# Mean squares from one product each, and convolution taps moved to earlier columns of the input projection

## What is computed

```python
def rmsnorm(x, g):
    xf = x.astype(jnp.float32)
    y = xf * lax.rsqrt(jnp.mean(xf * xf, axis=-1, keepdims=True) + RMS_EPS)
    return (y * g).astype(x.dtype)

ux = modulate(rmsnorm(x, norm1_g[l]), sh1, sc1) @ w_in[l]       # and uc from ctx
...                                                            # conformer_conv: 31 taps, depthwise;
...                                                            # rwkv: shift of 3 taps, key norm, scans
x = x + gt1 * (mix_x @ w_out[l])
x = x + gt2 * swiglu(modulate(rmsnorm(x, norm2_g[l]), sh2, sc2), ffn_wg[l], ffn_wu[l], ffn_wd[l])
```

## Time and profile before

| | |
|---|---|
| median of three runs | 4800.23 us |
| the profiled execution, its own time | 4803.96 us |
| its span in the profile | 4801.8 us |
| PE busy | 4443.0 us (93%) |
| DVE busy | 2203.6 us (46%) |
| ACT busy | 1320.5 us (27%) |
| POOL busy | 113.4 us (2%) |
| mean granted clock of TensorE | 0.958 of full speed |

### The profile page before, as it was taken

One profiled execution on the slowest core, in us unless ns is written; L12 is line 12 of the kernel. 1 busy time (PEld: TensorE's weight loads), 2 busy tenths in 40 slices (PEclk: granted clock), 3 DMA queues, 4 the chain that ended last, 5 costly groups with the idle time before them and its releaser, 6 DMA issues.

```text
span 4801.8 us, 81633 instructions
## 1 busy us (share of the span) xinstructions
PE 4443.0 (93%) x35773; PEld 3088.1 (64%) x35773; DVE 2203.6 (46%) x2957; ACT 1320.5 (27%) x1698; POOL 113.4 (2%) x107
## 2 busy tenths in 40 slices
PE   6997998899999998899889979898799999999996
PEld 3556997488855554899478536444466666666664
DVE  1566775232200255677244010345266666666663
ACT  2023223100000113322110021144254444444441
POOL 0000000000000000000000000000200000000000
PEclk9998999999999998999999989899799999999998
DMA  5330000111111332000222214100389999999995
GB/s 206 141 122 28 4 4 30 53 53 62 63 43 53 132 132 105 3 4 4 75 76 97 79 69 158 70 1 9 111 302 350 350 349 351 348 348 350 349 343 169
DMA packets 115465, 671.66 MB, mean 140 GB/s; under 512 B 11472, under 2 KB 12496, under 8 KB 57072
## 3 DMA queue, kind: packets, MB, share of 16 engines
q1 hardware_dynamic: 102496, 610.68, 33.7%
q0 software_dynamic: 12672, 56.48, 4.2%
HBM read 637.62 MB, written 30.68 MB: 139 GB/s over the span
## 4 chain that ended last, share of the span: by engine, by line
PE 83%; DVE 9%; ACT 3%; DMA 3%; issue 1%; POOL 0%; SPq 0%; DVEq 0%; ACTq 0%; POOLq 0%
PE psum L723 57%; PE psum L1280 14%; PE psum L1295 9%; DVE work L1429 1%; DMA ring<-w_in 1%; DMA ring<-stream 1%; DVE xt L1621 1%; PE psum L1273 1%; PE psum L1168 1%; PE psum L1254 1%; PE psum L1264 1%; DVE work L1915 1%; DVE ht L1399 0%; POOL places L661 0%; DVE ring_parts L2018 0%
## 5 line engine op out<-in xcount | busy, mean ns | idle before, releaser
L723 PE MATMUL psum<-ht,ring 128*128 128x512 f32 (+3 forms) x2368 | 825.2, 509 | 27.3 <-ACT ht L2148 14.1
L723 PE MATMUL psum<-work 64*64 64x64 f32 (+3 forms) x12552 | 683.1, 240 | 48.9 <-ACT work L2255 18.6
L723 PEld LDWEIGHTS psum<-ht,ring 128*128 128x128 f32 (+2 forms) x2368 | 437.8, 186 | 412.4 <-issue 374.1
L723 PEld LDWEIGHTS psum<-work 64*64 64x64 f32 (+2 forms) x12552 | 527.3, 139 | 154.5 <-issue 84.0
L723 PE MATMUL psum<-work,ring 128*128 128x512 f32 (+2 forms) x1488 | 458.0, 469 | 15.4 <-DMA ring<-stream 8.2
L723 PE MATMUL psum<-work_parts,ahead_parts 128*128 128x512 f32 (+1 forms) x1056 | 379.8, 360 | 31.1 <-DVE ht_parts L1788 31.1
L723 PEld LDWEIGHTS psum<-work,ring 128*128 128x128 f32 (+1 forms) x1488 | 258.7, 197 | 212.6 <-issue 199.2
L723 PE MATMUL psum<-work_parts,ring_parts 128*128 128x512 f32 (+1 forms) x1056 | 378.9, 359 | 0.0
L723 PE MATMUL psum<-ht_parts,ahead_parts 128*128 128x512 f32 (+1 forms) x1056 | 377.9, 358 | 0.0
L1750 DVE SCALAR_TENSOR_TENSOR xt<-psum,mod,xt 128x512 f32<-128x512 f32 x40 | 32.8, 820 | 555.0 <-PE psum L723 555.0
L1280 PE MATMUL psum<-work_parts 128*128 128x512 f32 x1024 | 278.6, 393 | 0.0
(11 more groups left out here) (285 smaller groups left out, 5418.6 us busy)
## 6 DMA issues: line engine op xcount, KB each, us to landing
ring<-stream SPq DMA_DIRECT2D x192, 1024.0 KB, 5.0
ring<-w_in SPq DMA_DIRECT2D x192, 1024.0 KB, 6.9
ht<-w_in SPq DMA_DIRECT2D x64, 1024.0 KB, 4.8
ht<-w_out SPq DMA_DIRECT2D x64, 1024.0 KB, 7.8
ring<-w_out SPq DMA_DIRECT2D x64, 1024.0 KB, 7.4
xt_rows<-xt POOLq DMA_DIRECT2D x2, 3132.0 KB, 13.8
xt<-xt_rows POOLq DMA_DIRECT2D x2, 3132.0 KB, 10.6
xt<-x_cm SPq DMA_DIRECT2D x8, 256.0 KB, 9.7
```

The costliest lines, as they stand in the source:

```text
L723: mm = pe.matmul(*args, **kwargs)
```

## The change

The squares of a norm are added up on VectorE (`add_square`), tile by tile in place into the first square; the squares behind it alternate between two tiles of the same buffer. TensorE makes one product of the sum. By-tile norms add square k-1 after the update of tile k, and the last one behind it. At the first norm ScalarE makes the squares after the first modulation turn, ahead of its work for the second row. The squares of a norm with context are taken over a tile's whole 783 columns in one operation. `EARLY_TAPS` goes from 20 to 36; the remaining 84 taps are spread over raw columns 0 to 11, seven each, and columns 12 to 15 have none.

```diff
-EARLY_TAPS = 20
+EARLY_TAPS, TAP_COLUMNS = 36, 12
...
+        sums_of = {"ht": [ht[:, i, :] for i in range(3)], "mix": [sq_mix[:, i, :] for i in range(3)],
+                   "attn": [sq_attn[:, i, :] for i in range(3)]}
...
-            def mean_square(with_ctx, squares):
-                by_tile("act", [(Cn("mean_dm"), squares[:, k, :]) for k in range(KT)], sq_act, with_ctx)
+            def mean_square(with_ctx, place):
+                pe.wait_ge(sq_added, w.next(sq_added, KT - 1))
+                j, stands, n_stands = banks.place("act")
+                if stands:
+                    pe.wait_ge(freed[stands], n_stands)
+                px, pc = halves(j)
+                total = sums_of[place][0]
+                if with_ctx:
+                    matmul(pc, Cn("mean_dm"), cs(total), start=True, stop=True)
+                for c in (0, CTX):
+                    mm = matmul(px[:, c:c + CTX], Cn("mean_dm"), xs(total)[:, c:c + CTX], start=True, stop=True)
+                mm.then_inc(ready["act"], 1)
...
+            def add_square(k, place, with_ctx):
+                total, *squares = sums_of[place]
+                f = whole(with_ctx)
+                dve.wait_ge(sq_act, w.next(sq_act, 2 if k == 1 else 1))
+                tt(f(total), f(total), f(squares[k % 2]), ALU.add).then_inc(sq_added, 1)
+                dve.wait_ge(sq_added, w.next(sq_added))
...
-                conv_taps(layer, EARLY_TAPS + late * n // 16, EARLY_TAPS + late * (n + 1) // 16)
+                first, last = (EARLY_TAPS + late * min(m, TAP_COLUMNS) // TAP_COLUMNS for m in (n, n + 1))
+                conv_taps(layer, first, last)
...
-            def add_gated(gate, layer, with_ctx, permuted):
+            def add_gated(gate, layer, with_ctx, permuted, place):
...
                     dve.sem_inc(x_tile, 1)
+                    if k >= 2:
+                        add_square(k - 1, place, with_ctx)
+                add_square(KT - 1, place, with_ctx)
...
-            def norm(shift, layer, with_ctx, squares, final=False, by_tile=True, modulations=0):
+            def squares(place, with_ctx, by_tile=True):
+                total, *temps = sums_of[place]
+                f = whole(with_ctx)
                 for k in range(KT):
                     if by_tile:
                         act.wait_ge(x_tile, w.next(x_tile))
-                    for f, b in parts(with_ctx):
-                        ins = fn(f(squares[:, k, :]), f(xt[:, k, :]), ACT.Square)
-                    ins.then_inc(sq_act, 1)
+                    if k >= 3:
+                        act.wait_ge(sq_added, w.next(sq_added))
+                    fn(f(temps[k % 2] if k else total), f(xt[:, k, :]), ACT.Square).then_inc(sq_act, 1)
...
                 mod_turn(0, q)
+                if q == 0:
+                    act.wait_ge(x_updated, 1)
+                    squares("ht", True, by_tile=False)
```

More of the change, by code:

```diff
@@ L356, in build @@
         x_tile = sem("x_tile")
+        sq_added = sem("squares_added")
         std_ready = sem("std_ready")
@@ L489, in cs, with whole @@
             return t[..., 0:CTX]
+        def whole(with_ctx):
+            return (lambda t: t) if with_ctx else xs
         def parts(with_ctx):
@@ L1082, in _ @@
             for layer in range(2):
-                mean_square(True, ht)
+                mean_square(True, "ht")
                 input_projection(layer)
@@ L1091, in _ @@
                 output_projection(layer == 0)
-                mean_square(layer == 0, sq_mix)
+                mean_square(layer == 0, "mix")
                 feed_forward(layer == 0)
             else:
-                mean_square(False, ht)
+                mean_square(False, "ht")
             def mods_after(slot):
@@ L1331, in _ @@
             output_projection_2()
-            mean_square(False, sq_attn)
+            mean_square(False, "attn")
             routing()
@@ L1827, in _ @@
                 if layer == 0:
+                    for k in range(1, KT):
+                        add_square(k, "ht", True)
                     modulation(0, 0, 2)
@@ L1840, in _ @@
                 dve.wait_ge(restored, 16 * (layer + 1))
-                add_gated(2, layer, layer == 0, True)
+                add_gated(2, layer, layer == 0, True, "mix")
                 updated()
@@ L1844, in _ @@
                 feed_forward(layer)
-                add_gated(5, layer, layer == 0, False)
+                add_gated(5, layer, layer == 0, False, "ht")
             updated()
@@ L2081, in _ @@
             modulation(2, 2, 6)
-            add_gated(2, 2, False, False)
+            add_gated(2, 2, False, False, "attn")
             updated()
@@ L2130, in norm @@
                         act.wait_ge(x_tile, w.next(x_tile))
-                    for f, b in parts(with_ctx):
-                        ins = fn(f(squares[:, k, :]), f(xt[:, k, :]), ACT.Square)
-                    ins.then_inc(sq_act, 1)
+                    if k >= 3:
+                        act.wait_ge(sq_added, w.next(sq_added))
+                    fn(f(temps[k % 2] if k else total), f(xt[:, k, :]), ACT.Square).then_inc(sq_act, 1)
+                w.skip(sq_added, 2)
+            def norm(shift, layer, with_ctx, place=None, final=False, modulations=0):
+                if place:
+                    squares(place, with_ctx)
                 if modulations:
@@ L2345, in _ @@
                 mod_turn(0, q)
+                if q == 0:
+                    act.wait_ge(x_updated, 1)
+                    squares("ht", True, by_tile=False)
             for layer in range(2):
-                if layer == 0:
-                    act.wait_ge(x_updated, 1)
-                norm(0, layer, True, ht, by_tile=layer > 0, modulations=1 + layer)
+                norm(0, layer, True, "ht" if layer else None, modulations=1 + layer)
                 act.wait_ge(zeroed, w.next(zeroed))
@@ L2360, in _ @@
                     banks.pair("dve")
-                norm(3, layer, layer == 0, sq_mix)
+                norm(3, layer, layer == 0, "mix")
                 feed_forward(layer == 0)
@@ L2365, in _ @@
             else:
-                norm(0, 1, False, ht, final=True)
+                norm(0, 1, False, "ht", final=True)
             def mods_after(slot):
@@ L2539, in _ @@
             fn(lam[:, 2:4], lam[:, 0:2], ACT.Exp).then_inc(lam_exp, 1)
-            norm(0, 2, True, ht, modulations=2)
+            norm(0, 2, True, "ht", modulations=2)
             projections()
@@ L2544, in _ @@
                 banks.pair("dve")
-            norm(3, 2, False, sq_attn)
+            norm(3, 2, False, "attn")
             routing()
```

## The result

The changed kernel takes **4748.74 us** (median of 4 runs, 4745.4 to 4749.44) beside 4800.34 us for the kernel before on the same chip; the ratio is 0.9893, with a 95% interval from 0.9881 to 0.9906. That is 51.6 us less; 56.7 were forecast. The profiled execution has 4749.44 us of its own, 0.7 above its median, while that of before was 3.6 above its own (4803.96 against 4800.34); so the two spans differ by more than the medians, 54.5 us (4801.8 and 4747.3), and the following reading accounts for that difference.

The account below looks back on a forecast made before the run. TensorE, with 83% of the chain, was taken to bound the kernel, through its work and its waits. Norms 27.1, layer 0's columns 15.6 and layer 1's 14.0 sum to 56.7 us off 4800.2: 4743.5 us, range 4732 to 4761.

Parts of the forecast that it names:

- The first norm: First norm: squares paced by adds, second modulation turn late at the low clock, product ends at 59.2, not 65.3: gain 6.1 us.
- Adds: VectorE's adds of squares over 783 columns at norms with context: 1.02 us taken for each.
- Norms with context by tile: Layer 0's mix norm and layer 1's start: TensorE waits 3.4 us, short product 2.93 us; gains 4.0 and 4.1 us.
- Norms without context: Layer 1's mix norm, final norm, attention norm: wait 2.4 us, product about 1.1 us; 3.4 us each, 10.2 together.
- Early taps: Layer 0: 34 taps take 32.3 us and end before the next gated value is due; nothing waits, cost 0.
- Layer 0's columns: End of layer 0's projection: tapless columns 12 to 15 lose their waits, despite pauses at columns 8 and 10: gain 15.6 us.
- the first rival: Layer 0's added pauses at columns 8 and 10 lower the clock, 3.0 us each: gain 50.7, 4749.5 us; chance 0.10.
- Layer 1's columns: End of layer 1's projection: waits of 2.03 and 4.10 us and the low clock go: gain 14.0 us.
- The second rival: The key chain, not taps, sets TensorE's waits; only the last column's taps count: gain 38.5, 4761.7 us; chance 0.08.
- Nothing lost behind a norm: Stages behind each norm run no longer than before, loss 0; longer ones would show the prediction wrong.

Follow-up runs that it names:

- experiment 2: Kernel before the change with only the new spread of taps (36 early, 7 in each of columns 0 to 11), old norms: 4772.24 us.
- experiment 3: Changed kernel with ScalarE making the first norm's squares before the copies of both modulation rows: 4738.91 us.
- experiment 9: The changed kernel run once more, unaltered, in a later job: 4742.43 us.
- experiment 4: Changed kernel with 8 taps in each of columns 0 to 7 and 5 in 8 to 11, instead of 7 in all twelve: 4741.38 us.
- experiment 7: Changed kernel with 36 early taps but the other 84 spread over all 16 columns: 4764.88 us.
- experiment 10: The kernel of experiment 8 (changed kernel with 20 early taps, the rest in columns 0 to 11) run again beside the changed kernel: 4747.0 us.
- experiment 1: Changed kernel with the taps as before (20 early, the rest over 16 columns), so the norms alone: 4774.62 us.
- experiment 5: Changed kernel with the edits of experiment 3 and experiment 4 together: 4737.08 us.
- experiment 6: Kernel of experiment 5 plus two rounds of products of constants on TensorE while it waits at the five by-tile norms: 4738.54 us.
- experiment 8: Changed kernel with 20 early taps and the other 100 in columns 0 to 11 (8 or 9 each): 4746.16 us.
- experiment 11: The kernel of experiment 5 run again beside the changed kernel: 4736.0 us.

## Why the prediction was right

It gave 4743.5 us, from 4732 to 4761, and faster with a chance of 0.97; the two medians, 4748.7 and 4742.4, lie on both sides of it. The mechanism held stage by stage. That the total came so close is in part luck: the first norm and layer 0's columns gave 1.1 us more each and the second block's context came 2.1 sooner, while the three norms without context gave 2.1 less, layer 1's columns 0.7 less, and a stage with no edit in it lost 2.4. By its steps:

- **The first norm**, 6.1 forecast, 7.2 measured. The late turn at the low clock came as worked out (3.57 us where 3.6 stood). The adds paced ScalarE at 1.01 us and not 1.03, and its copies began at 50.51 us and not behind 51.2.
- **Adds.** 1.02 us was taken; the mean is 975 ns, and 1.0 in a chain. The waits of 3.44 and 2.5 to 2.8 us came where 3.4 and 2.4 were forecast.
- **Norms with context by tile**, 4.0 and 4.1 forecast, 4.6 and 4.2 measured: the mean product took 2.38 and 2.71 us, not the 2.93 that was taken, since the clock came down inside it (granted 1.00 until 915 us, 0.54 in the next).
- **Norms without context**, 10.2 forecast, 8.1 measured. This is the term that was sized wrongly. The step that failed is "about 1.1 us (two thirds of 1.56) at the full clock, since 2.4 is near 2.03": the product took 1.14, 1.72 and 2.07 us in the three, and the waits were 0.1 to 0.4 us longer than 2.4. The prediction had named this case ("At the low clock 0.9 less each").
- **Early taps**, cost 0 forecast. The 34 taps take 32.22 us (32.3 forecast) and end at 144.96, and the next gated value still waits for TensorE, not the reverse. Timeline of DVE after:

```profile
112.74 32.22 DVE L1456 SCALAR_TENSOR_TENSOR work<-work,vec 128x783 f32<-128x783 f32 x34
...
147.25 0.69 DVE L1443 TENSOR_TENSOR work<-psum,work 128x512 f32<-128x512 f32 x1 [2.29 <-PE psum L731]
```

- **Layer 0's columns**, 15.6 forecast, 16.7 measured. The pauses of 1.57 and 1.8 us came as 1.58 and 1.70 and left the clock up, as forecast, and so they did in the three other traces that have them (experiments 2, 3 and 9): the first rival falls. Counted from the projection's start, they delayed product 20 by 1.9 us and not by 2.75: TensorE came to the first of them 0.9 us sooner, as its first product took 22.57 us where that of before took 23.46, partly at the low clock. The rest, from product 22 to the recurrence, brought 8.2 us where 8.1 were forecast. The prediction takes the turn at 1.8 us where its row says 1.95; the stretch that it is part of, from the key product of column 12 to product 22, came out at the 5.15 us that were worked out.
- **Layer 1's columns**, 14.0 forecast, 13.3 measured: a wait of 0.59 us for the key sum stayed, where 0.2 was taken, and the first product took 22.94 us where it took 22.53 before.
- **The second rival**, a chain on ScalarE that paces the keys, falls by experiments 2, 4 and 7: with fewer taps ahead of them the keys' waits go, tap by tap.
- **Nothing lost behind a norm** was wrong. It was one of the prediction's own signs of being wrong ("if the stages behind each norm run longer than before"), and stages behind the norms lost some 5 us in the first pair of traces, of which 2.4 lie ahead of the mix norm of layer 0. The change touches nothing there. In the windows from TensorE's start behind its wait of 11.5 us to the first update of the output projection, of before, after, and experiment 10 (first column the window, PEclk the granted clock):

```profile
core 0: us, PE busy (x) PEld busy (x) DVE busy (x) ACT busy (x) POOL busy (x), PEclk, DMA share, GB/s
828.07:860.45 32.38, 31.22 (x81) 15.01 (x82) 12.03 (x24) 0.00 (x0) 0.00 (x0) 0.94 0.17 65
```

```profile
804.55:838.88 34.33, 33.17 (x81) 15.82 (x82) 12.12 (x25) 0.00 (x0) 0.00 (x0) 0.88 0.16 62
```

```profile
809.07:841.28 32.21, 31.05 (x81) 14.87 (x82) 12.03 (x24) 0.00 (x0) 0.00 (x0) 0.95 0.17 66
```

The same work takes 2 us more where the granted clock is 0.88 and not 0.94. Most of it is a second stretch at the low clock within the stage. All thirteen traces have a pause of 1.16 us there, ahead of the output projection's first product; behind it, before and after:

```profile
849.78:852.78 3.00, 3.00 (x7) 1.40 (x8) 0.00 (x0) 0.00 (x0) 0.00 (x0) 1.00 0.28 44
```

```profile
826.70:829.70 3.00, 3.00 (x4) 1.45 (x5) 0.00 (x0) 0.00 (x0) 0.00 (x0) 0.50 0.00 0
```

Of the thirteen traces three have the short form, 32.1 to 32.4 us (before, experiments 2 and 10), and ten the long one, 34.1 to 34.5 us (the changed kernel twice, experiments 1, 3 to 8 and 11). Experiments 8 and 10 are one kernel, so the form isn't fixed by the code. But both kernels with the old norms have the short one and ten of the eleven traces with the new norms the long one, so a part of the edit in it isn't excluded. Why the clock falls in one execution and not in another stays open, and so does the cause of the 1.3 us lost at the end.

The rule of the Trainium skill that was weighed (page "TensorE: Matmul & The Clock Gate", Part 1: an idle array falls to 1.2 GHz and gets 2.4 back after sustained work) would have put all seven products low if every pause counted as idle, as the prediction took it. The rows are between: all those with context came out low wholly or in part (2.38, 2.71, 2.91, 2.93 us against 1.56), of the three others one came out at the full clock (1.14 us).

## What to carry to other kernels

Where an engine off the path has slack, the question is not how much of it but where it stands when the path asks for it: the taps taken off the last 4 of 16 raw columns and put on the first 12 and further ahead were worth 30 us in two layers by the traces (16.7 + 13.3), with no work removed. Replacing long products by adds on another engine wins the products' length less the last two adds and one short product, often at the low clock. What the engines had done under the long product has to be looked at anew (here the modulation copies, 5.6 us). Check such edits of a few us in the trace, stage by stage: medians of one kernel differed by 6 us between jobs.

## What the runs showed of the hardware

- A pause of TensorE is priced twice, by its length and by the clock behind it, and its length alone doesn't tell the second. Pauses up to 2.03 us left the key products at 1.53 to 1.56 us in every trace; one of 2.91 gave 2.33; one of 3.46 gave 2.67 (2.93 in the repetition), and those of 4.92 and 4.94 gave 2.93. But the mean products without context, one form, took 1.14, 1.72 and 2.07 us behind 2.81, 2.49 and 2.48 us within one execution, and a pause of 1.16 us ahead of layer 0's output projection had the clock at 0.50 behind it in ten traces and at 1.00 in three. Part of the products ahead of that pause use 32 rows of the array (`32*128`, a row of the timeline after at 819.81 us); whether the fall there comes from them or from the pause no run tells.
- The fall needn't come within the pause: behind 3.44 us the granted clock was still 1.00 when the product started and fell about 0.6 us into it (changed kernel, mix norm of layer 0).
- Once the same form came out at 1.57 us after a pause of 3.44 (experiment 10, mix norm of layer 0), where the nine other traces with this norm and this pause had 2.31 to 2.46 us. Its row:

```profile
916.89 1.57 PE L731 MATMUL psum<-work,con 128*128 128x256 f32 x6 [3.44 <-DVE work L1414]
```

- The clock can be held up by products of constants in the pause: 1.57 us at both norms with context and a granted clock of 1.00 (experiment 6, one trace).
